# Low halves of the MLP down weights by an accumulating transfer instead of GpSimd subtractions

## The chip, the cores and the metric

The kernel runs on one core of a Trainium2 chip. The metric is the device time of one execution in microseconds; the number for a kernel is the median of its runs.

## The reference, cut to what matters

Two model blocks run in sequence on 512 tokens of width 1024, all in fp32. The first is attention with a gated convolution, a gated feed-forward part and an embedding gate. The second has two layers; each is a mixer (retention in the first, chunked attention in the second) followed by a squared-relu MLP with a hidden width of 4096. The change touches these two MLPs alone:

```
def _sqrelu_mlp(h, w1, w2):
    u = jax.nn.relu(h @ w1)
    return (u * u) @ w2
...
    for i in range(DEPTH_2):
...
        h = h + _sqrelu_mlp(_rmsnorm(h, mlp_norm_g[i]), mlp_w1[i], mlp_w2[i])
```

Every matrix product is made in nearly full fp32 precision out of three products of rounded parts. A number is split into a high part, rounded to fp32r, and a low part, the rest. The kernel adds high times high, high times low and low times high.

## The kernel before, in words

**Chunks and slots.** Weights are streamed in chunks of 1 MB (128 partitions x 2048 columns). Each chunk has a slot, its number modulo 2, in three buffers: `raw` (as loaded), `w_hi` (the high part) and `w_lo` (the low part). Four engines and queues handle a chunk in turn:

- SyncE loads it into `raw` (`load`, L495, issue at L501). It first waits until the low part of the chunk two before, which used the same slot, is made (L498).
- ScalarE copies `raw` to `w_hi`, which rounds it (`split`, L1333, the copy at L1338). It waits for the load and until TensorE has done the group that read the slot before (`two_before`).
- GpSimd subtracts: `w_lo = raw - w_hi`, in four instructions of 512 columns (`lo`, L649, L654). It waits for `w_hi_ready` and counts up `w_lo_ready`.
- TensorE waits for `w_lo_ready` (`chunk_ready`, L715) and makes 48 matmuls of 512 columns: 8 slices of the contraction, 2 output tiles, 3 products (`product`, L738; the matmuls are L729, L730 and L731). With the last of a group it counts up `group_done`.

**The MLP.** A layer's MLP runs over 4 groups (`MLP_GROUPS`), each with 8 chunks. Chunks 0 to 3 are slices of `w1` ("up"): each gives two tiles of the hidden activations, so 8 tiles in all. Chunks 4 to 7 are slices of `w2` ("down"): each contracts all 8 hidden tiles and gives two output tiles, which VectorE adds to `x` (L2039). TensorE's order is `mlp`, L1212. In the first down chunk of a group it waits before each slice k for hidden tile k (`mlp_lo`, L1225).

**ScalarE's order** is written out by hand in `mlp`, L1849. After up group m it splits chunk m + 2, then makes the squares (L1861) and rounds them to the high hidden part (L1864), two tiles each. `down_splits`, L1867, then splits chunks 6 to 9, where 8 and 9 are the up chunks 0 and 1 of the next group. In the last group the splits of chunks 6 and 7 stand between the work for the next norm (L1882 to L1884).

**VectorE** takes relu times the norm factor out of PSUM (L2648) and, after ScalarE, makes the low hidden part by a subtraction (L2652).

**GpSimd's order** is the order of the chunks. From the third chunk of the retention layer on it is one loop over pairs of chunks to the end (L704 to L710):

```
            with pool.Fori(0, after) as i:
                lo(first + 2 * i, first % 2)
                lo(first + 1 + 2 * i, (first + 1) % 2)
```

The waits of one chunk are in the helper `Chunk` (`loads`, `two_before`), those of PSUM in `Group`.

Of the kernel before, what the change touches and what calls it, by code (L numbers as in the profile page):

```python
# [22 lines left out]
F32 = mybir.dt.float32  # L23
F32R = mybir.dt.float32r
I32 = mybir.dt.int32
ALU = mybir.AluOpType
ACT = mybir.ActivationFunctionType
# [33 lines left out]
MLP_GROUPS = 4  # L61
# [80 lines left out]
RET = Phase(GATE, [1, 1, 1, 1, 1, 1, 2, 2], RH)  # L142
MLP_A = Phase(RET, [1] * 8, MLP_GROUPS)

ATT_ORDER = [(kind, g) for kind, g in zip("qkvqkvqkvqkvoooo", (0, 0, 0, 1, 1, 1, 2, 2, 2, 3, 3, 3, 0, 1, 2, 3))]
ATT = Phase(MLP_A, [4 if kind == "o" else 1 for kind, _ in ATT_ORDER])
# [21 lines left out]
class Norm:  # L168
# [39 lines left out]
 ret_v_mean ret_v_lo ret_sq ret_acc ret_var ret_ln ret_rstd ret_ys ret_gate ret_y ret_y_hi ret_y_lo  # L208
 two_s two_mx two_nmx two_exp two_rs two_p two_t two_hi two_lo two_pv two_shift two_o two_ohi two_olo
 gain_pair ffn_old_hi ffn_old_lo apart_done apart_scaled apart_sum gate_old_hi gate_old_lo gate_old_done gate_e_hi gate_e_lo gate_sig gate_read  # L210
 mlp_sq mlp_hi mlp_lo att_in_hi att_in_lo tab_scaled ffn_silu ffn_part fin_tmp fin_t fin_half fin_left fin_right""".split()


def build(nc, T, out):
# [3 lines left out]
    with ExitStack() as ctx:  # L218
# [412 lines left out]
        @block.gpsimd  # L631
        def _(pool):
            pool.memset(ones[:, :], 1.0).then_inc(s["memset_done"], 1)
            pool.memset(eps[:, :], EPS).then_inc(s["memset_done"], 1)

            kr_raw = aux[:, 0, :].rearrange("p (k c) -> p k c", k=KD)
            w_in = T["w_in"][0].rearrange("(k p) c -> p k c", p=P)
            at = Q_RANK + KV_RANK
            pool.wait_ge(s["first_in0"], 32)
            pool.dma_start(tab[:, 0, :].bitcast(I32), bass.AP(T["positions"].tensor, 0, [[0, P], [1, S]]))\  # L640
                .then_inc(s["pos_in"], 16)
            pool.dma_start(freq[:, :], T["c_freq"]).then_inc(s["pos_in"], 16)
            pool.wait_ge(raw_ready[1], MIX.chunk(1).loads)
            for dst, src, n in ((0, 0, 32), (32, 16, 16), (48, 0, 16)):
                pool.dma_start(kr_raw[:, :, dst:dst + n], w_in[:, :, at + src:at + src + n])\
                    .then_inc(s["kr_in"], 16)
            pool.dma_start(ext[:, 255:255 + REL_TABLE], T["att_rel_bias_2"][0]).then_inc(s["ext_in"], 16)

            def lo(number, slot, parts=False, quarters=4):  # L649

                pool.wait_ge(s["w_hi_ready"], number + 1)
                for n in range(quarters):
                    at = slice(n * 512, n * 512 + 512)
                    ins = pool.tensor_tensor(w_lo[:, slot, at], raw[:, slot, at], w_hi[:, slot, at].bitcast(F32),  # L654
                                             ALU.subtract)
                    if parts and n < 3:
                        ins.then_inc(s["w_part"], 1)
                ins.then_inc(s["w_lo_ready"], 1)

            pool.wait_ge(s["w_lo_ready"], 2)  # L660
            lo(MIX.chunk0 + 2, (MIX.chunk0 + 2) % 2)

            pool.wait_ge(s["w_lo_ready"], UQ.chunk0)
            pool.wait_ge(s["w_hi_ready"], UQ.chunk0 + 1)
            for w_lo_part, w_hi_part, raw_part in uq_parts():
                ins = pool.tensor_tensor(w_lo_part, raw_part, w_hi_part.bitcast(F32), ALU.subtract)
            ins.then_inc(s["w_lo_ready"], 1)

            def conv_scaled(half):

                xv = CONV_X[half]
                for m in range(2):
                    pool.wait_ge(pair_free[xv.pair], xv.freed(m))
                    if half == 0 and m == 0:
                        pool.wait_ge(s["r_squared"], 1)
                    u = conv_u[2 * half + m]
                    pool.tensor_tensor(u, u, r_squared, ALU.mult).then_inc(s["conv_ur"], 1)

            for n in range(CONVS.chunks):
                if n == 2:  # L680
                    conv_scaled(0)
                lo(CONVS.chunk0 + n, (CONVS.chunk0 + n) % 2)
                if n == 3:
                    conv_scaled(1)
            lo(WOUT.chunk0, WOUT.chunk0 % 2)
            for m in range(2):
                pool.wait_ge(pair_free[CONV_B[0].pair], CONV_B[0].freed(m))
                pool.tensor_tensor(conv_u[m], conv_u[m], rstd[:, :], ALU.mult).then_inc(s["conv_out0"], 1)
            lo(WOUT.chunk0 + 1, (WOUT.chunk0 + 1) % 2)
            lo(WOUT.chunk0 + 2, WOUT.chunk0 % 2, parts=True)  # L690
            lo(WOUT.chunk0 + 3, (WOUT.chunk0 + 1) % 2)
            lo(PROJ.chunk0, PROJ.chunk0 % 2)
            for n in range(3):
                lo(FFN.chunk0 + n, (FFN.chunk0 + n) % 2, parts=n == 2)
            first = FFN.chunk0 + 3
            before = (FFN_LAST.chunk0 + 6 - first) // 2
            with pool.Fori(0, before) as i:
                lo(first + 2 * i, first % 2)
                lo(first + 1 + 2 * i, (first + 1) % 2)
            for c in range(first + 2 * before, GATE.chunk0 + 4):  # L700
                lo(c, c % 2, parts=c == GATE.chunk0 + 2, quarters=3 if 6 <= c - FFN_LAST.chunk0 < 10 else 4)
            lo(RET.chunk0, RET.chunk0 % 2)
            pool.wait_ge(s["w_lo_ready"], RET.chunk0 + 2)
            first = RET.chunk0 + 2  # L704
            after = (N_CHUNKS - first) // 2
            with pool.Fori(0, after) as i:
                lo(first + 2 * i, first % 2)
                lo(first + 1 + 2 * i, (first + 1) % 2)
            for c in range(first + 2 * after, N_CHUNKS):
                lo(c, c % 2)  # L710


        @block.tensor
# [618 lines left out]
        def _(act):  # L1332
            def split(c, columns=CH):  # L1333

                act.wait_ge(raw_ready[c.slot], c.loads)
                if not c.early:
                    act.wait_ge(s["group_done"], c.two_before)
                act.activation(w_hi[:, c.slot, 0:columns], raw[:, c.slot, 0:columns], ACT.Copy)\  # L1338
                    .then_inc(s["w_hi_ready"], 1)

            def group_ready(g):
                act.wait_ge(s["group_done"], g.done)

# [505 lines left out]
            def mlp(ph, norm, base, next_norm, next_gain):  # L1849
                def up(i, first=False):  # L1850
                    for m in range(4):
                        g = ph.group(m, i)
                        group_ready(g)
                        split(ph.chunk(m + 2, i))
                        if first and m == 0:
                            rsqrt(norm, D)
                        if m:
                            act.wait_ge(s["mlp_lo"], base + i * 8 + 2 * m)
                        for t in range(2):
                            act.wait_ge(pair_free[g.pair], g.freed(t))  # L1860
                            act.activation(tmp[:, t, :], sq[:, t, :], ACT.Square).then_inc(s["mlp_sq"], 1)  # L1861
                        for t in range(2):
                            act.wait_ge(s["mlp_sq"], base + i * 8 + 2 * m + t + 1)
                            act.activation(hid_hi[:, 2 * m + t, :], tmp[:, t, :], ACT.Copy)\  # L1864
                                .then_inc(s["mlp_hi"], 1)

                def down_splits(i):  # L1867
                    for m in range(4):
                        split(ph.chunk(6 + m, i))

                up(0, first=True)
                down_splits(0)
                with act.Fori(1, MLP_GROUPS - 1) as i:
                    up(i)
                    down_splits(i)
                i = MLP_GROUPS - 1
                up(i)
                for m in range(4):
                    g = ph.group(4 + m, i)
                    if next_gain or m < 3:  # L1880
                        group_ready(g)
                    following = ph.chunk(6 + m, i) if m < 2 or next_gain else None  # L1882
                    if following and m < 3:
                        split(following)  # L1884
                    for t in range(2):
                        act.wait_ge(pair_free[g.pair], g.freed(t))
                        if next_gain:
                            gained_hi(next_norm, 2 * m + t, (next_gain[0], next_gain[1] + 2 * m + t))
                        square(next_norm, 2 * m + t, x[:, 2 * m + t, :])
                    if following and m == 3:  # L1890
                        split(following)
# [974 lines left out]
```

## Time and profile before

| | |
|---|---|
| three runs | 1994.1, 1995.39, 1995.42 us |
| median | 1995.39 us |
| profiled execution, span from first to last instruction | 1992.5 us |
| the same with what lies around the span | not recorded apart; the three runs are 1.6 to 2.9 us above the span |
| busy: TensorE, VectorE, ScalarE, GpSimd | 1975.0, 974.1, 782.6, 915.7 us |
| first MLP, about | 1058 to 1400 us of the span |
| second MLP, about | 1643 to 1975 us of the span |

PE is TensorE, PEld its weight loads, DVE VectorE, ACT ScalarE, POOL GpSimd, SP SyncE; a q behind a name is that engine's queue. L12 is line 12 of the kernel. Matmuls are pipelined: a matmul's row lasts 0.39 us while the next one starts 0.22 to 0.23 us after it. Rows of a timeline that stand for several instructions merge them: the duration runs from the first's start to the last's end.

### The profile page before, as it was taken

The numbers are of one execution on the slowest core, as the hardware profiler recorded it, in microseconds if no ns is written. First come the engines' busy times: TensorE is split into PE (matmuls) and PEld (weight loads), VectorE is DVE, ScalarE is ACT, GpSimd is POOL, SyncE is SP. The second block draws the span as 40 slices with busy tenths as digits, with TensorE's granted clock in tenths as the row PEclk, the third lists the DMA queues.
The fourth block names the chain that finished last, engine by engine and source line by source line (L and its number), as shares of the span: only waits on it lengthen the run. The fifth ranks groups of instructions, "written<-read, shape, count | busy, mean of one in ns | idle before, by whom it ended". The sixth has DMA issues, their size and how long they took to land.

```text
span 1992.5 us, 24116 instructions
## 1 busy us (share of the span) xinstructions
PE 1975.0 (99%) x9360; PEld 1640.7 (82%) x9360; DVE 974.1 (49%) x1447; ACT 782.6 (39%) x1137; POOL 915.7 (46%) x662
## 2 busy tenths in 40 slices
PE   8999999999999999999999999999999999999998
PEld 7877878888888888888888888888888888888887
DVE  7667753432358745454555131325466783132234
ACT  7546442321235443434354132233455553223232
POOL 2433555545455344444445454545333345454552
PEclk9999999999999999999999999999999999999999
DMA  5312367375322313232323323233222223323231
GB/s 162 93 49 69 116 94 123 88 101 114 100 90 85 127 64 106 65 104 68 101 66 103 100 90 106 84 105 105 84 84 85 94 74 106 106 85 105 92 98 64
DMA packets 165555, 187.05 MB, mean 94 GB/s; under 512 B 3992, under 2 KB 152224, under 8 KB 165344
## 3 DMA queue, kind: packets, MB, share of 16 engines
q1 hardware_dynamic: 163632, 181.61, 28.6%
q10 hardware_dynamic: 1584, 3.74, 4.2%
q8 instruction: 58, 0.95, 0.2%
q0 software_dynamic: 256, 0.55, 0.1%
q14 instruction: 25, 0.20, 0.0%
HBM read 180.77 MB, written 4.72 MB: 93 GB/s over the span
## 4 chain that ended last, share of the span: by engine, by line
PE 92%; DVE 3%; issue 2%; ACT 1%; POOL 1%; DMA 1%; DVEq 0%; SPq 0%; POOLq 0%; ACTq 0%
PE ps L729 29%; PE ps L730 29%; PE ps L731 29%; PE ps L931 1%; PE ps L901 1%; POOL w_lo L654 1%; PE ps L940 1%; PE ps L941 1%; PE ps L918 1%; ACT w_hi L1338 0%; DMA freq<-in_c_freq 0%; DVE hn_lo L2481 0%; DVE x L2476 0%; DVE scr L1983 0%; ACT scr L1540 0%
## 5 line engine op out<-in xcount | busy, mean ns | idle before, releaser
L654 POOL TENSOR_TENSOR w_lo<-raw,w_hi 128x512 fp32r<-128x512 f32 x636 | 897.1, 1442 | 989.1 <-ACT w_hi L1338 989.1
L729 PE MATMUL ps<-hn_hi,w_hi 128*128 128x512 f32 x1524 | 600.4, 394 | 2.3 <-DVE hn_lo L2328 1.7
L1338 ACT ACTIVATE w_hi<-raw 128x2048 fp32r<-128x2048 f32 (+1 forms) x162 | 308.9, 1907 | 735.5 <-PE ps L731 735.4
L730 PE MATMUL ps<-hn_lo,w_hi 128*128 128x512 f32 x1524 | 593.4, 389 | 0.0
L731 PE MATMUL ps<-hn_hi,w_lo 128*128 128x512 f32 x1524 | 593.4, 389 | 0.0
L730 PE MATMUL ps<-hid_lo,w_hi 128*128 128x512 f32 x904 | 351.7, 389 | 0.0
L729 PE MATMUL ps<-hid_hi,w_hi 128*128 128x512 f32 x888 | 347.0, 391 | 0.1
L731 PE MATMUL ps<-hid_hi,w_lo 128*128 128x512 f32 x888 | 345.6, 389 | 0.0
L729 PEld LDWEIGHTS ps<-hn_hi,w_hi 128*128 128x128 f32 x1524 | 286.2, 188 | 67.4 <-issue 3.5
L731 PEld LDWEIGHTS ps<-hn_hi,w_lo 128*128 128x128 f32 x1524 | 286.1, 188 | 60.4
L730 PEld LDWEIGHTS ps<-hn_lo,w_hi 128*128 128x128 f32 x1524 | 286.3, 188 | 58.9 <-issue 1.4
L2039 DVE TENSOR_TENSOR x<-ps,x 128x512 f32<-128x512 f32 x128 | 82.5, 686 | 278.3 <-PE ps L731 278.2
L730 PEld LDWEIGHTS ps<-hid_lo,w_hi 128*128 128x128 f32 x904 | 169.7, 188 | 35.0 <-issue 0.2
L729 PEld LDWEIGHTS ps<-hid_hi,w_hi 128*128 128x128 f32 x888 | 166.7, 188 | 36.7 <-DVE hid_lo L2428 0.8
L731 PEld LDWEIGHTS ps<-hid_hi,w_lo 128*128 128x128 f32 x888 | 166.7, 188 | 35.0
L2652 DVE TENSOR_TENSOR hid_lo<-scr,hid_hi 128x512 fp32r<-128x512 f32 x64 | 100.9, 1615 | 72.2 <-ACT hid_hi L1864 72.2
L2648 DVE SCALAR_TENSOR_TENSOR scr<-ps,scr 128x512 f32<-128x512 f32 x64 | 41.2, 686 | 154.3 <-PE ps L731 145.4
L2032 DVE TENSOR_TENSOR scr<-ps,scr 128x512 f32<-128x512 f32 x42 | 27.1, 686 | 138.7 <-PE ps L731 135.3
L729 PE MATMUL ps<-w_hi,hn_hi 128*128 128x512 f32 (+1 forms) x256 | 87.0, 340 | 0.2 <-DVE scr L2556 0.2
L730 PE MATMUL ps<-w_lo,hn_hi 128*128 128x512 f32 (+1 forms) x256 | 86.0, 336 | 0.0
L731 PE MATMUL ps<-w_hi,hn_lo 128*128 128x512 f32 (+1 forms) x256 | 86.0, 336 | 0.0
L1983 DVE TENSOR_TENSOR scr<-scr 128x512 f32<-128x512 f32 x65 | 67.3, 1035 | 13.3 <-ACT scr L1358 9.7
(322 smaller groups left out, 1882.9 us busy)
## 6 DMA issues: line engine op xcount, KB each, us to landing
raw<-in_mlp_w SPq DMA_DIRECT2D x64, 1024.0 KB, 5.3
raw<-in_ret_w_in SPq DMA_DIRECT2D x24, 1024.0 KB, 5.1
raw<-in_att_w_in SPq DMA_DIRECT2D x12, 1024.0 KB, 5.2
raw<-in_w_gate SPq DMA_DIRECT2D x11, 1024.0 KB, 5.4
raw<-in_w_up SPq DMA_DIRECT2D x11, 1024.0 KB, 5.3
raw<-in_w_down SPq DMA_DIRECT2D x8, 1024.0 KB, 8.0
raw<-in_ret_w_out SPq DMA_DIRECT2D x8, 1024.0 KB, 5.1
raw<-in_w_in SPq DMA_DIRECT2D x7, 1024.0 KB, 5.7
```

The costliest lines, as they stand in the source:

```text
L654: ins = pool.tensor_tensor(w_lo[:, slot, at], raw[:, slot, at], w_hi[:, slot, at].bitcast(F32), ALU.subtract)
L729: pe.matmul(o, hi, rhs_hi, start=start, stop=False, skip_group_check=True)
L730: pe.matmul(o, hi, rhs_lo, start=False, stop=False, skip_group_check=True)
L731: return pe.matmul(o, lo, rhs_hi, start=False, stop=stop, skip_group_check=True)
L901: ins = pe.matmul(a.score_ps(b, t), q[:, t * P:(t + 1) * P], k[:, 0:(t + 1) * P], start=(n == 0), stop=(n == last), skip_group_check=True)
L918: ins = pe.matmul(a.score_ps(b, t), q[:, t * P:(t + 1) * P], k[:, 0:(t + 1) * P], start=(nth == 0 and n == 0 and t != 0), stop=(nth == 1 a ...
L1338: act.activation(w_hi[:, c.slot, 0:columns], raw[:, c.slot, 0:columns], ACT.Copy)\
L1983: dve.tensor_tensor(ssq, ssq, squares[:, t % 2, :], ALU.add).then_inc(s["norm_acc"], 1)
L2032: dve.tensor_tensor(dst, ps[:, g.bank(m), :], r, ALU.mult).then_inc(pair_free[g.pair], 1)
L2039: dve.tensor_tensor(dst, ps[:, g.bank(m), :], dst, ALU.add).then_inc(pair_free[g.pair], 1)
L2648: dve.scalar_tensor_tensor(sq[:, t, :], ps[:, g.bank(t), :], 0.0, r_bc, ALU.max, ALU.mult).then_inc(pair_free[g.pair], 1)
L2652: dve.tensor_tensor(hid_lo[:, 2 * m + t, :], tmp[:, t, :], hid_hi[:, 2 * m + t, :].bitcast(F32), ALU.subtract)\
```

## The change

For the down chunks (4 to 7 of each MLP group, 32 chunks in all) ScalarE makes two copies: the high part as before, and the high part negated into `w_lo`. GpSimd then issues one transfer that adds `raw` to `w_lo` (1 MB, inside SBUF), waits until it has landed, and counts up `w_lo_ready` itself. Up chunks and all other chunks keep the subtractions. GpSimd's one loop becomes a loop up to the first MLP, the first MLP written out, a loop over the attention layer, and the second MLP written out.

```diff
@@ GpSimd
-            first = RET.chunk0 + 2
-            after = (N_CHUNKS - first) // 2
-            with pool.Fori(0, after) as i:
-                lo(first + 2 * i, first % 2)
-                lo(first + 1 + 2 * i, (first + 1) % 2)
-            for c in range(first + 2 * after, N_CHUNKS):
-                lo(c, c % 2)
+
+            def lo_pairs(first, last):
+
+                with pool.Fori(0, (last - first) // 2) as i:
+                    lo(first + 2 * i, first % 2)
+                    lo(first + 1 + 2 * i, (first + 1) % 2)
+
+            def lo_by_dma(c, nth):
+
+                pool.wait_ge(s["w_hi_ready"], c.number + 1)
+                pool.dma_start(w_lo[:, c.slot, :].bitcast(F32), raw[:, c.slot, :], accum_op=ALU.add)\
+                    .then_inc(s["lo_landed"], 16)
+                pool.wait_ge(s["lo_landed"], 16 * nth)
+                pool.wait_ge(s["w_lo_ready"], c.number)
+                pool.sem_inc(s["w_lo_ready"], 1)
+
+            def mlp_lo(ph, layer):
+
+                for i in range(MLP_GROUPS):
+                    for m in range(4):
+                        lo(ph.chunk0 + m + 8 * i, ph.chunk(m).slot)
+                    for m in range(4):
+                        lo_by_dma(ph.chunk(4 + m, i), 4 * MLP_GROUPS * layer + m + 1 + 4 * i)
+
+            lo_pairs(RET.chunk0 + 2, MLP_A.chunk0)
+            mlp_lo(MLP_A, 0)
+            lo_pairs(ATT.chunk0, MLP_B.chunk0)
+            mlp_lo(MLP_B, 1)
@@ ScalarE
+            def split_negated(c):
+
+                act.wait_ge(raw_ready[c.slot], c.loads)
+                act.wait_ge(s["group_done"], c.two_before)
+                act.activation(w_hi[:, c.slot, :], raw[:, c.slot, :], ACT.Copy)
+                act.activation(w_lo[:, c.slot, :], raw[:, c.slot, :], ACT.Copy, scale=-1.0).then_inc(s["w_hi_ready"], 1)
@@ ScalarE, mlp: after up group m
-                        split(ph.chunk(m + 2, i))
+                        (split if m < 2 else split_negated)(ph.chunk(m + 2, i))
@@ ScalarE, mlp: down_splits
-                        split(ph.chunk(6 + m, i))
+                        (split_negated if m < 2 else split)(ph.chunk(6 + m, i))
@@ ScalarE, mlp: last group
-                        split(following)
+                        (split_negated if m < 2 else split)(following)
```

One semaphore, `lo_landed`, is added to the list.

## Rows read from the trace of the kernel before

**Rows 1.** The page's span, and its busy times of each engine.

```profile
span 1992.5 us, 24116 instructions
...
PE 1975.0 (99%) x9360; PEld 1640.7 (82%) x9360; DVE 974.1 (49%) x1447; ACT 782.6 (39%) x1137; POOL 915.7 (46%) x662
```

**Rows 2.** Busy times by window, the two MLP stages.

```profile
core 0: us, PE busy (x) PEld busy (x) DVE busy (x) ACT busy (x) POOL busy (x), PEclk, DMA share, GB/s
...
1065.00:1410.00 345.00, 345.00 (x1528) 285.77 (x1527) 113.41 (x114) 104.78 (x117) 174.66 (x125) 1.00 0.31 100
...
1650.00:1950.00 300.00, 300.00 (x1325) 248.40 (x1324) 87.82 (x90) 87.39 (x94) 150.34 (x109) 1.00 0.31 98
```

**Rows 3.** Timeline around a chunk border: start us, us, engine, line, what.

```profile
1112.46 0.39 PE L731 MATMUL ps<-hid_hi,w_lo 128*128 128x512 f32 x1
1112.46 0.19 PEld L729 LDWEIGHTS ps<-hid_hi,w_hi 128*128 128x128 f32 x1
1112.68 0.39 PE L729 MATMUL ps<-hid_hi,w_hi 128*128 128x512 f32 x1
...
1112.94 1.92 ACT L1338 ACTIVATE w_hi<-raw 128x2048 fp32r<-128x2048 f32 x1 [8.96 <-PE ps L731]
```

**Rows 4.** Timelines of ScalarE, GpSimd and SyncE's queue, one down chunk; GpSimd beside VectorE.

```profile
1102.07 1.92 ACT L1338 ACTIVATE w_hi<-raw 128x2048 fp32r<-128x2048 f32 x1 [6.86 <-PE ps L731]
...
1104.06 5.02 POOL L654 TENSOR_TENSOR w_lo<-raw,w_hi 128x512 fp32r<-128x512 f32 x4 [4.92 <-ACT w_hi L1338]
...
1109.25 0.37 SPq L501 DMA_DIRECT2D raw<-in_mlp_w  x1
...
1093.20 5.94 POOL L654 TENSOR_TENSOR w_lo<-raw,w_hi 128x512 fp32r<-128x512 f32 x4 [4.94 <-ACT w_hi L1338]
```

**Rows 5.** Timeline of ScalarE, a split and the instruction right behind it.

```profile
1035.90 1.92 ACT L1338 ACTIVATE w_hi<-raw 128x2048 fp32r<-128x2048 f32 x1 [4.36 <-PE ps L731]
1037.72 0.71 ACT L1383 ACTIVATE hn_hi<-x,gains 128x512 fp32r<-128x512 f32 x1
```

**Rows 6.** Timelines of ScalarE and VectorE, chunk 5's split and the last hidden tiles.

```profile
1091.21 1.92 ACT L1338 ACTIVATE w_hi<-raw 128x2048 fp32r<-128x2048 f32 x1 [6.88 <-PE ps L731]
...
1094.72 3.27 DVE L2652 TENSOR_TENSOR hid_lo<-scr,hid_hi 128x512 fp32r<-128x512 f32 x2 [2.30 <-ACT hid_hi L1864]
```

**Rows 7.** Timeline of VectorE, two such subtractions while GpSimd is idle.

```profile
1027.87 1.29 DVE L2606 TENSOR_TENSOR hid_lo<-o_buf,hid_hi 128x512 fp32r<-128x512 f32 x2
```

**Rows 8.** SyncE's loads (L501) in the first MLP: ns min/median/max, and landing.

```profile
L501 SPq DMA_DIRECT2D raw<-in_mlp_w x28: 372/372/373, 1066.0 to 1360.4; - x28
...
DMA to landing us min/median/max: 5.0/5.2/5.8
```

**Rows 9.** DMA queue, 1065 to 1410 us: packets, MB, share of 16 engines.

```profile
q1 hardware_dynamic: 33771, 34.40, 31.4%
```

**Rows 10.** Busy times by short windows after the load issue at 1109.25.

```profile
1109.00:1111.00 2.00, 2.00 (x10) 1.65 (x10) 0.00 (x0) 0.00 (x0) 0.08 (x1) 1.00 0.31 50
1111.00:1113.00 2.00, 2.00 (x11) 1.65 (x10) 0.11 (x1) 0.06 (x1) 0.00 (x0) 1.00 1.01 332
1113.00:1115.00 2.00, 2.00 (x11) 1.65 (x10) 1.18 (x2) 1.86 (x1) 0.06 (x1) 1.00 0.41 143
```

**Rows 11.** DMA issues of the whole run: count, KB each, median us to landing.

```profile
hid_hi<-hid_hi SPq DMA_DIRECT2D x3, 64.0 KB, 2.0
...
aux<-in_w_in POOLq DMA_DIRECT2D x1, 128.0 KB, 3.0
```

**Rows 12.** Timeline of GpSimd, its DMA issues at the start.

```profile
5.92 0.75 POOL L640 DMA_DIRECT2D tab<-in_positions  x1 [4.93 <-DMA raw<-in_w_in]
...
16.47 2.67 POOL L645 DMA_DIRECT2D aux<-in_w_in  x3 [9.26 <-DMA raw<-in_w_in]
```

**Rows 13.** Busy times by window, the first and the last microseconds.

```profile
0.00:6.00 6.00, 0.60 (x3) 0.51 (x4) 0.00 (x0) 1.75 (x3) 0.53 (x7) 1.00 0.66 208
...
1985.00:1992.00 7.00, 0.27 (x3) 0.03 (x1) 2.45 (x4) 1.90 (x4) 0.00 (x0) 0.87 0.75 300
```

More of the change, by code:

```diff
@@ L210 @@
  gain_pair ffn_old_hi ffn_old_lo apart_done apart_scaled apart_sum gate_old_hi gate_old_lo gate_old_done gate_e_hi gate_e_lo gate_sig gate_read
- mlp_sq mlp_hi mlp_lo att_in_hi att_in_lo tab_scaled ffn_silu ffn_part fin_tmp fin_t fin_half fin_left fin_right""".split()
+ mlp_sq mlp_hi mlp_lo lo_landed att_in_hi att_in_lo tab_scaled ffn_silu ffn_part fin_tmp fin_t fin_half fin_left fin_right""".split()
 def build(nc, T, out):
```

## The prediction

> **What bounds the kernel now.** I began with the busy time of each engine [rows 1]: TensorE is busy for 1975.0 us of a span of 1992.5, every other engine for half or less. The table by stage [rows 2] says where the missing 17.5 us lie: not in the two MLP stages. From 1065 to 1410 us TensorE is busy for 345.00 of 345.00 us, from 1650 to 1950 for 300.00 of 300.00, at a granted clock of 1.00 (its 2.4 GHz level). So a faster GpSimd, VectorE or ScalarE can give nothing back inside the MLP stages; the change can only be hidden or cost time, and what decides is how much room each step has before TensorE must wait.
>
> The rhythm is read in the timeline around one chunk border [rows 3, 4]. Matmuls start every 0.2265 us, 48 of them make a chunk, and ScalarE's split starts at 1102.07 and again at 1112.94: one chunk is 10.87 us. With the split's start as zero: the high weights are there at 1.92, GpSimd starts at 1.99 and ends at 7.01, SyncE issues the next load at 7.18. TensorE's first weight load of the next chunk starts at 1112.46, that is at 10.39. GpSimd's four subtractions take 5.02 us there, and 5.94 where VectorE works beside them [rows 4]; the room today is 3.4 us or 2.5 us. Nothing is late now, and the change replaces 5 to 6 us of GpSimd by a second pass of ScalarE and a transfer.
>
> **The change, part by part.** It touches chunks 4 to 7 of each of the 4 groups of each of the 2 MLPs, 32 chunks.
>
> *GpSimd's subtractions go*: 32 times 5.0 to 5.9 us, all of it beside TensorE's work. Worth nothing on the path.
>
> *ScalarE's second pass comes*: another 128x2048 copy of 1.92 us. Two such neighbours on ScalarE overlap a little, the next instruction starts 1.82 us after a split's start [rows 5]. So the negated copy ends at 1.82 + 1.92 = 3.74, and GpSimd, which follows a split's end by 0.07 to 0.08 us [rows 4], issues the transfer at 3.82. What waits behind it on ScalarE: for chunk 5 the squares and high halves of the last up group. They, and VectorE's low halves behind them, move by 1.82 us. Today that chain starts at 1091.21 and ends with VectorE's two subtractions from 1094.72 to 1097.99 [rows 6], 6.8 us after the split's start. TensorE needs the hidden tile 6 after 36 matmuls, and tile 7 after 42, that is 8.15 and 9.5 us into the chunk (times 0.2265), or 7.9 and 9.25 after the split's start, which follows the chunk's first matmul by 0.26 us [rows 3]. With 1.82 us more tile 6 is there at about 7.0 and tile 7 at 8.6. Room of 0.65 us or more is left even at VectorE's present 1.64 us for each, and with GpSimd idle they may fall back to the 0.65 us a piece (1.29 for two) of a stretch where it is idle [rows 7]. Cost nothing. In the down part ScalarE idles 8.96 us before each split [rows 3], which covers the pass.
>
> *The accumulating transfer comes.* It reads 1 MB of raw, reads and writes 1 MB of w_lo. No row shows an adding transfer. The nearest rows are the loads of the same size: in the first MLP 5.2 us from issue to landing, 372 ns of it in SyncE's queue [rows 8]. One load's data pass in 0.62 + 2.02 + 0.82 = 3.5 us of the 16 engines' time (share times 2 us in the three short windows [rows 10]); the queue's 31.4% of 345 us over 34.40 MB gives 3.3 us for 1 MB [rows 9], so some 1.9 us are fixed. The 64 KB copies inside SBUF landed in 2.0 us, so the fixed part is no smaller there [rows 11]. A transfer from GpSimd costs more to issue: 0.75 us and 2.67 us for three, against 0.37; one of 128 KB landed in 3.0 us [rows 11, 12], that is 2.6 fixed after 0.4 of data. I take 2.4. The lower bound has the second read hidden beside the first: 2.4 + 3.3 = 5.7 us. The upper one has three passes in turn, two reads and a write: 2.4 + 9.9 = 12.3 us. I take two passes, since a copy too has one read and one write and shows one pass: 2.4 + 6.6 = 9.0 us.
>
> The Trainium skill (Collectives: The Full Stack, "The bandwidth ceiling") says that a reducing transfer runs at half the rate of a copy, because it needs two source reads on one ring. The load rows bear on it only as the price of a copy. By its own figure for a copy, 31 GB/s per engine, halved and times 16, 1 MB would take an estimated 4.2 us instead of 6.6, and the whole change would come to about 5 us.
>
> *What the room allows.* The transfer must have landed before 10.39, less 0.2 us for two semaphore hops (GpSimd, then TensorE; SyncE takes 0.17 us after GpSimd's end for one [rows 4]): 10.19 − 3.82 = 6.37 us. With 9.0 us the overshoot is 2.63 us.
>
> *How often it is paid.* Not 32 times. There are two slots. If chunk 4 starts 2.63 us late, TensorE is still at it 2.63 us longer, but the split of chunk 5 started when chunk 3 ended, before that wait. GpSimd is free when chunk 4's transfer has landed, 1.9 us into that split (12.82 − 10.87), before the negated copy is done. So chunk 5's transfer starts on time and finds a deadline moved by 2.63 us: no wait. Chunk 6's split starts at the end of chunk 4 and pays again. A pair of chunks costs one overshoot. 16 pairs: 16 × 2.63 = 42 us.
>
> *Loads beside transfers.* SyncE's load for the same slot now waits for the landing. In the second chunk of a pair it is issued 2.1 us after the split's start (12.82 + 0.17 − 10.87) and moves data from 1.15 to 4.6 us later [rows 4, 10], so till 6.7, while the transfer's data start at about 5.3. The overlap is 1.4 us per pair, worth 0 to 22 us in all. I take 0, because two full passes is already the dear side of the two nearest prices. The load itself lands at about 7.3 and is wanted by the next split, at 13.5: hidden. GpSimd's wait has only its own next chunk behind it; after chunk 7 comes an up chunk with 5.0 to 5.9 us of subtraction, started at once or up to the overshoot late, within 10.39.
>
> Sum against the profiled execution: 1992.5 + 42 = 2034.6 us of span. The runs shown are 1994.1 to 1995.42, median 1995.39, 2.9 us over the span, and 1995.39 + 42.1 = 2037.5 us. A measurement of this kernel can tell about 0.2%, 4 us, from no change.
>
> **The rivals.**
>
> *A: the transfer fits.* The second read hides or inner rows of 8 KB move faster than the loads' 1 KB pieces, and landing comes within 6.37 us, or within 0.25 us of it (16 × 0.25 = 4). For it: 5.7 us, the lower bound, is inside. Against it: it asks for almost the time of a plain load with a second megabyte read. Time: 1995.4 us. It ends on the other side: not slower. It decides at 6.37 us of issue to landing. Chance 0.17.
>
> *B: the skill's rate.* 2.4 + 4.2 = 6.6 us (worked from the page named above); by rows alone any price between 6.6 and 7.5 us does the same: 16 × 0.25 to 16 × 1.1, 1999 to 2013 us. Chance 0.16.
>
> *C: dearer than two passes.* With 12.3 us the overshoot is 5.93. Then GpSimd's order bites: chunk 5's transfer can't start before 16.2, lands at 28.5, TensorE ends chunk 4 at 27.2, and the pair costs 7.4 us: 119 us, 2114 us. Still slower adding would make each chunk cost the transfer alone. For it: nothing here shows the adding. Chance 0.14.
>
> *D: the clock falls in the new gaps.* After TensorE stopped at the end, the granted clock of the last 7 us was 0.87, a mix of its two levels, 2.4 and 1.2 GHz; in the first 6 us, with 0.6 us of work, it was 1.00 [rows 13]. Gaps of 2.6 us between 20 us of dense work look like the second. If it fell at each gap for half a chunk, 5.4 us each and 87 us in all would come on top: about 2125 us. Chance 0.03.
>
> *E: faster.* Only stretches with idle TensorE could give, and none of those holds a down chunk. Chance 0.03.
>
> **How the numbers follow.** Two passes, with a landing from 7.5 to 11 us: 0.47, 2013 to about 2080 us. So slower 0.47 + 0.16 + 0.14 + 0.03 = 0.80, same 0.17, faster 0.03. The range goes from A's time with the runs' own spread, 1993, to the three passes, 2115; left out are E's part, half of C and most of D, together under 0.2. The likeliest case alone spans 2013 to 2080.
>
> **What would show it.** In the changed profile: 32 accumulating issues on GpSimd with their time to landing, 9.0 us if right, under 6.4 under A. Splits' starts in the down part 13.5 us apart and 10.9 us apart in turn, not all alike. TensorE's busy time in the first MLP unchanged at 345 us beside about 21 us of idle time, released by GpSimd or its queue. The copies L1338 counted 162 as before plus 32 negated ones of 1.9 us. VectorE's hid_lo subtractions shorter where GpSimd is idle, with no gain from it. The prediction is wrong if the landing is under 6.4 us, if each chunk and not each pair pays, if the loads stretch the transfers by more than 1.4 us, or if the granted clock leaves 1.00.

## The result and the profile after

The changed kernel takes 2009.62 us (median of 4 runs, 2008.16 to 2010.71), the kernel before 1995.41 us beside it: a ratio of 1.007, interval 1.0058 to 1.0082, so 14.2 us slower. Slower was right and 2009.6 lies in the range (a wide one, 1993 to 2115), but the forecast was 2037.5: the loss is a third of the 42 us expected.

The page of the changed kernel: span and busy times (as [rows 1]), the transfers among the costliest groups, and their issues (as [rows 11]).

```profile
span 2007.3 us, 23957 instructions
...
PE 1981.2 (99%) x9360; PEld 1640.3 (82%) x9360; DVE 930.8 (46%) x1447; ACT 839.7 (42%) x1169; POOL 762.4 (38%) x566
...
L714 POOL DMA_DIRECT2D w_lo<-raw x32 | 27.7, 866 | 302.0 <-ACT w_lo L1367 302.0
...
w_lo<-raw POOLq DMA_DIRECT2D x32, 1024.0 KB, 7.0
```

GpSimd lost 153 us of work and VectorE 43; neither shows in the time. TensorE's waits in the changed kernel name the place (who waited for whom: us in total, times, longest):

```profile
PE ps L750 <- POOLq L718: 8.5, 16, 1.7
```

L718 is GpSimd's count-up after the landing. Sixteen waits, not 32: 15 at the first chunk of a pair, and one at a second chunk, whose transfer took 7.6 us. They are 0.5 us each as idle time. The rest of the 14.8 us of span is added busy time, 1981.2 against 1975.0 us: a matmul's row counts 0.39 to 0.50 us on either side of a wait, where a step in the stream is 0.23. The windows of the two MLPs (as [rows 2]) are now short of full by 3.3 and 3.9 us:

```profile
1065.00:1410.00 345.00, 341.74 (x1497) 279.90 (x1496) 90.64 (x113) 131.96 (x129) 95.97 (x76) 1.00 0.54 146
...
1650.00:1950.00 300.00, 296.07 (x1298) 242.79 (x1296) 70.92 (x90) 108.53 (x104) 88.12 (x69) 1.00 0.52 140
```

The timeline of ScalarE shows the rhythm of one group, chunks 4 to 7 and then 8 (only the splits' first copies are copied here):

```profile
1081.25 1.92 ACT L1366 ACTIVATE w_hi<-raw 128x2048 fp32r<-128x2048 f32 x1 [6.88 <-PE ps L752]
...
1092.13 1.92 ACT L1366 ACTIVATE w_hi<-raw 128x2048 fp32r<-128x2048 f32 x1 [5.08 <-PE ps L752]
...
1103.70 1.92 ACT L1366 ACTIVATE w_hi<-raw 128x2048 fp32r<-128x2048 f32 x1 [5.77 <-PE ps L752]
...
1114.58 1.92 ACT L1366 ACTIVATE w_hi<-raw 128x2048 fp32r<-128x2048 f32 x1 [7.16 <-PE ps L752]
...
1126.10 1.92 ACT L1359 ACTIVATE w_hi<-raw 128x2048 fp32r<-128x2048 f32 x1 [7.80 <-PE ps L752]
```

The spacings are 10.88, 11.57, 10.88 and 11.52 us: one late start per pair of chunks, as the prediction's two-slot argument had it. The transfer between them, and where TensorE stands when it lands (timelines of GpSimd and of all engines):

```profile
1107.71 0.86 POOL L714 DMA_DIRECT2D w_lo<-raw  x1 [10.68 <-ACT w_lo L1367]
...
1114.09 0.39 PE L752 MATMUL ps<-hid_hi,w_lo 128*128 128x512 f32 x1
...
1114.78 0.19 PEld L750 LDWEIGHTS ps<-hid_hi,w_hi 128*128 128x128 f32 x1 [0.73 <-POOLq L718]
```

Issue at 4.01 us after the split's start, landing 7.0 later, weight load at 1114.78 − 1103.70 = 11.08 instead of 10.39 [rows 3]: an overshoot of 0.69 us. 16 × 0.69 = 11.0. In the profiled executions the first MLP takes 346.2 us (1059.65 to 1405.84, from the split of chunk 1 to a split behind the last group) against 340.1. The second takes 321.6 us (1650.74 to 1972.33, from the split of chunk 1 to the last split) against 315.3, and what follows the last split takes 1.5 us more: 13.9 us in all. The other 0.9 of the 14.8 us of span lie ahead of the first down chunk; the start varies by such an amount from kernel to kernel (the same split stands between 1058.44 and 1060.61 us in the ten profiles of this study).

What 11.0 leaves of the 13.9 us goes with four late landings of 7.6, 8.3, 7.8 and 7.9 us; the other 28 took 6.9 to 7.0. Beside three of the four the instruction queue moved 16 KB while the transfer was under way, and beside none of the 28; the fourth (7.8 us) follows the one of 8.3, which had moved a load onto it. The DMA queues from 1787.2 to 1795.5 us, the time of the longest one (packets, MB, share of 16 engines):

```profile
q0 software_dynamic: 144, 1.05, 62.5%
q8 instruction: 1, 0.02, 1.1%
```

That the one causes the other is not shown: no run moved the instruction queue's packets, and with the plain copy below one transfer had such company and was on time.

### The profile page after: what moved, and what is told of

Its sections match the earlier page's. It is cut to its first block and busy times, and to the rows that moved or that the text cites. A ratio compares the mean times of both kernels' runs of the same rounds, so it can differ in the third digit from the quotient of the medians.

```text
span 2007.3 us, 23957 instructions
## 1 busy us (share of the span) xinstructions
PE 1981.2 (99%) x9360; PEld 1640.3 (82%) x9360; DVE 930.8 (46%) x1447; ACT 839.7 (42%) x1169; POOL 762.4 (38%) x566
## 5 line engine op out<-in xcount | busy, mean ns | idle before, releaser
L654 POOL TENSOR_TENSOR w_lo<-raw,w_hi 128x512 fp32r<-128x512 f32 x508 | 716.2, 1440 | 849.9 <-ACT w_hi L1359 849.9
L1359 ACT ACTIVATE w_hi<-raw 128x2048 fp32r<-128x2048 f32 (+1 forms) x130 | 247.3, 1902 | 495.8 <-PE ps L752 495.7
L1366 ACT ACTIVATE w_hi<-raw 128x2048 fp32r<-128x2048 f32 x32 | 61.4, 1917 | 196.4 <-PE ps L752 196.4
L714 POOL DMA_DIRECT2D w_lo<-raw x32 | 27.7, 866 | 302.0 <-ACT w_lo L1367 302.0
L2680 DVE TENSOR_TENSOR hid_lo<-scr,hid_hi 128x512 fp32r<-128x512 f32 x64 | 69.1, 1120 | 100.9 <-ACT hid_hi L1892 100.9
```

Of the source, the lines that this page charges most:

```text
L714: pool.dma_start(w_lo[:, c.slot, :].bitcast(F32), raw[:, c.slot, :], accum_op=ALU.add)\
L1366: act.activation(w_hi[:, c.slot, :], raw[:, c.slot, :], ACT.Copy)
L2680: dve.tensor_tensor(hid_lo[:, 2 * m + t, :], tmp[:, t, :], hid_hi[:, 2 * m + t, :].bitcast(F32), ALU.subtract)\
```

## The experiments

Each kernel is compared with the kernel before in the same session. Edits are against the changed kernel.

**Negated copy first.** GpSimd's transfer needs the negated low buffer and raw, not the high buffer. (The semaphore memset_done stands at 2 since the start and is counted on.)

```diff
-act.activation(w_hi[...], raw[...], ACT.Copy)
-act.activation(w_lo[...], raw[...], ACT.Copy, scale=-1.0).then_inc(s["w_hi_ready"], 1)
+act.activation(w_lo[...], raw[...], ACT.Copy, scale=-1.0).then_inc(s["memset_done"], 1)
+act.activation(w_hi[...], raw[...], ACT.Copy).then_inc(s["w_hi_ready"], 1)
...
-pool.wait_ge(s["w_hi_ready"], c.number + 1)
+pool.wait_ge(s["memset_done"], 2 + nth)
 pool.dma_start(w_lo[...], raw[...], accum_op=ALU.add).then_inc(s["lo_landed"], 16)
 pool.wait_ge(s["lo_landed"], 16 * nth)
+pool.wait_ge(s["w_hi_ready"], c.number + 1)
```

> Edit of the changed kernel: ScalarE makes the negated low copy first and the high copy second, and GpSimd issues the transfer after the first of the two; everything else, all 32 transfers included, stays. Theory (the only loss is landing minus room): the issue comes at about 2.0 us after the split's start instead of 4.0, so a landing of 7.0 us ends at about 9.0, inside the 10.2 us of room. No split is spaced 11.5 us any more, TensorE is busy throughout both MLPs, time 1995 to 1997 us. Rival (the transfers disturb TensorE, the loads or the queues by themselves): a part of the 14 us stays, 2002 us or more.

Measured: 1997.46 us, ratio 1.0006 (0.9997 to 1.0015). The changed kernel's 14 us are gone with all 32 transfers in place; only when they start has changed. The windows of the two MLPs (busy times):

```profile
1065.00:1410.00 345.00, 345.00 (x1527) 286.00 (x1526) 90.91 (x114) 133.49 (x133) 98.41 (x77) 1.00 0.55 148
...
1650.00:1950.00 300.00, 299.30 (x1321) 247.68 (x1320) 70.69 (x88) 111.77 (x107) 86.37 (x69) 1.00 0.54 144
```

TensorE is full again, but for two waits behind late landings (median 6.9 us, longest 9.1):

```profile
PE ps L751 <- POOLq L719: 0.9, 2, 0.7
```

The theory holds: the loss was landing minus room.

**Chunks 4 and 6 by transfer, and chunks 4 and 5.** Sixteen transfers each; the other down chunks are subtracted as before the change, and ScalarE negates only where a transfer follows. The second kernel has `m < 2` where the first has `m % 2 == 0`.

```diff
 for m in range(4):
-    lo_by_dma(ph.chunk(4 + m, i), ...)
+    if m % 2 == 0:
+        lo_by_dma(ph.chunk(4 + m, i), ...)
+    else:
+        lo(ph.chunk0 + 4 + m + 8 * i, ph.chunk(4 + m).slot)
```

> Only the first chunk of each pair, 4 and 6, goes by the transfer (16 transfers); 5 and 7 are subtracted by GpSimd as before the change. Theory (a pair of chunks pays one overshoot, the second chunk starts in time): the same loss as with all 32, 16 x 0.69 = 11 us, time 2006 to 2009 us, with splits spaced 11.5 and 10.9 in turn. Rival (each transfer costs its share): half, about 2002 us.

> Only chunks 4 and 5, one pair per group, go by the transfer (16 transfers, as many as with 4 and 6); 6 and 7 are subtracted. Theory (one overshoot per pair): 8 x 0.69 = 5.5 us, 2000 to 2003 us. Rival (each transfer costs the same wherever it stands): the same time as the kernel with chunks 4 and 6.

Measured: with 4 and 6, 2008.33 us, ratio 1.0062 (1.0046 to 1.0077); with 4 and 5, 2002.51 us, ratio 1.0035 (1.0023 to 1.0047). That is 12.4 and 6.5 us over before, for the same number of transfers. TensorE's waits in the two, first 4 and 6, then 4 and 5:

```profile
PE ps L753 <- POOLq L718: 7.6, 16, 1.7
```

```profile
PE ps L753 <- POOLq L718: 3.7, 9, 0.5
```

Half the transfers in the right places cost nearly all of the loss, and half of them packed into pairs cost half. The nine waits are one for each of the eight pairs and one at the second chunk whose transfer again took 7.6 us. The pair pays, not the transfer.

**A plain copy.** The addition is left out, so the low part is not the rest of the weights.

```diff
-pool.dma_start(w_lo[...], raw[...], accum_op=ALU.add)
+pool.dma_start(w_lo[...], raw[...])
```

> The transfer is a plain copy of raw onto the low buffer, of the same size and from the same queue, without the addition (so the low part is wrong and the addition is left out). The term that was mis-sized is the transfer's data part, 5 us instead of 6.6. Theory P (the pass in SBUF is quicker than a load's, and the addition is two such passes): the copy's data take about half of 5 us and it lands in 4.3 to 4.8 us. Rival Q (the pass costs as much as a load's, 3.3 us, and the second read is partly hidden): it lands in 5.2 to 5.5 us. Either way it is inside the room of 6.3 us and the time is that of the kernel before, 1995 to 1997 us.

Measured: 1995.66 us, ratio 0.9999 (0.9989 to 1.0008). Its issues (L714: ns min/median/max) and landings, and its share of the queues from 1065 to 1410 us (16 transfers of 1 MB; packets, MB, share of 16 engines; q1 is SyncE's loads, q0 GpSimd's transfers):

```profile
L714 POOL DMA_DIRECT2D w_lo<-raw x32: 527/528/599, 1084.2 to 1964.4; - x32
...
DMA to landing us min/median/max: 4.4/4.5/6.4
...
q1 hardware_dynamic: 33817, 34.45, 31.5%
q0 software_dynamic: 2304, 16.78, 12.6%
```

The same three views of the changed kernel:

```profile
L714 POOL DMA_DIRECT2D w_lo<-raw x32: 859/859/929, 1085.3 to 1976.3; - x32
...
DMA to landing us min/median/max: 6.9/7.0/8.3
...
q1 hardware_dynamic: 32880, 33.49, 29.8%
q0 software_dynamic: 2304, 16.78, 24.1%
```

12.6% of 345 us in 16 parts is 2.7 us of data for a copy, 24.1% is 5.2 us for an addition: 1.9 times the copy. Taken from the landings of 4.5 and 7.0 us, both leave 1.8 us, called the fixed part here. So theory P was right: doubling was the right rule, the price of a pass and the fixed part were not. The Trainium skill's half rate (Collectives: The Full Stack, "The bandwidth ceiling") is what the trace shows, 24.1 against 12.6; its 31 GB/s per engine, given there for a collective's ring, is not: 1 MB in 2.7 us on 16 engines is 24 GB/s.

**Half the columns added.** The low part of the other half is left out.

```diff
-pool.dma_start(w_lo[:, c.slot, :]..., raw[:, c.slot, :], accum_op=ALU.add)
+pool.dma_start(w_lo[:, c.slot, 0:1024]..., raw[:, c.slot, 0:1024], accum_op=ALU.add)
```

> Only the first 1024 of the 2048 columns are added; the low part of the other half is left out. Landing time at half the size. If the fixed part is 1.8 us and the data part 5.2 us for 1 MB: 4.4 us. If the fixed part is the predicted 2.4 us with 4.6 us of data: 4.7 us. Inside the room either way: 1995 to 1997 us.

Measured: 1996.2 us (one run). Landings, and the queue's share from 1065 to 1410 us:

```profile
DMA to landing us min/median/max: 4.5/4.5/5.8
...
q0 software_dynamic: 2304, 8.39, 12.8%
```

12.8% for 16 half transfers is 2.8 us each: 1.7 us fixed, against 1.8 for the whole transfer. The two expectations, 4.4 and 4.7, are too near each other for the landing alone to decide; the share does.

**Two halves, pipelined.** ScalarE makes high and negated parts of one half, then of the other; GpSimd issues a transfer behind each and waits for both at the end.

```diff
+for h in range(2):
+    at = slice(h * 1024, h * 1024 + 1024)
+    act.activation(w_hi[:, c.slot, at], raw[:, c.slot, at], ACT.Copy)
+    act.activation(w_lo[:, c.slot, at], raw[:, c.slot, at], ACT.Copy, scale=-1.0)\
+        .then_inc(s["w_hi_ready" if h else "memset_done"], 1)
```

> ScalarE works by halves of 1024 columns (high, negated, high, negated) and GpSimd issues a transfer behind each half, without waiting between them. Theory: the first half is issued at about 2.1 us and its data are done by 6 us, the second is issued at about 4.1 and lands 4.4 us later, or at most 1 us more behind the first: 8.5 to 9.5 us, inside the room of 10.2. No loss, 1995 to 1998 us, the same as with the negated copy first. Rival (each transfer has a cost of its own, 64 issues of 0.9 us and 64 landings): a part of the 14 us stays or it gets more, 2003 us or over.

Measured: 1996.26 us, ratio 1.0003 (0.9994 to 1.0012). A second way to start earlier removes the loss as well, with 64 issues instead of 32; no price of the transfers themselves shows as long as they land in time. Neither repair beats the kernel before.

**Two halves in turn.** This gives the forecast its own conditions: a landing of about 9 us.

```diff
+for h in range(2):
+    at = slice(h * 1024, h * 1024 + 1024)
+    pool.dma_start(w_lo[:, c.slot, at]..., raw[:, c.slot, at], accum_op=ALU.add).then_inc(s["lo_landed"], 16)
+    pool.wait_ge(s["lo_landed"], 32 * nth - 16 + 16 * h)
```

> The transfer is made in two halves of 1024 columns, the second issued only when the first has landed. This puts a landing of about the predicted 9.0 us in place of 7.0: two times 1.8 us fixed and 2.6 us of data, 8.9 us with the wake-up between. Theory (a pair pays one overshoot, loads beside transfers cost little): overshoot 2.6 us, splits spaced 13.5 and 10.9 us in turn, 16 x 2.6 = 42 us, time 2036 to 2040 us. Rival (at this size each chunk pays, or the loads stretch the second transfer of each pair by the overlap of 1.4 us): 2060 us or more for all 32, or 2050 to 2060 us with spacings of 13.5 and 12. Rival (the clock falls in gaps of 2.6 us): a granted clock under 1.00 in the MLPs and over 2060 us.

Measured: 2074.68 us, ratio 1.0384 (1.0368 to 1.04): 79 us, not 42. The theory fails here, and both rivals have their part. Timeline of GpSimd, issues of chunk 4's two halves, chunk 5's two halves:

```profile
1084.24 0.93 POOL L716 DMA_DIRECT2D w_lo<-raw  x1 [6.97 <-ACT w_lo L1369]
1089.15 0.88 POOL L716 DMA_DIRECT2D w_lo<-raw  x1 [3.98 <-DMA w_lo<-raw]
1095.10 0.86 POOL L716 DMA_DIRECT2D w_lo<-raw  x1 [5.07 <-ACT w_lo L1369]
1101.79 0.86 POOL L716 DMA_DIRECT2D w_lo<-raw  x1 [5.83 <-DMA w_lo<-raw]
```

Chunk 4's first half takes 4.9 us to the next issue, chunk 5's takes 6.7: its landing is 6.4 us instead of 4.5, beside a load that SyncE issued at 1093.93, when chunk 4 had landed. Timeline of TensorE at that landing, and windows from there on (the granted clock is the third figure from the end):

```profile
1090.59 0.39 PE L754 MATMUL ps<-hn_hi,w_lo 128*128 128x512 f32 x1
1093.82 0.50 PE L752 MATMUL ps<-hid_hi,w_hi 128*128 128x512 f32 x1 [2.85 <-POOLq L720]
```

```profile
1094.00:1096.00 2.00, 2.00 (x7) 1.64 (x8) 0.00 (x0) 2.00 (x4) 0.86 (x1) 0.72 0.45 114
1096.00:1098.00 2.00, 2.00 (x6) 1.54 (x6) 1.29 (x2) 0.89 (x2) 0.00 (x0) 0.50 1.03 350
1098.00:1100.00 2.00, 2.00 (x10) 1.60 (x9) 0.00 (x0) 0.00 (x0) 0.00 (x0) 0.93 1.10 245
```

After a gap of 2.85 us the granted clock is 0.72, 0.50 and 0.93 in the next three windows: 1.2 GHz for part of the chunk, and 6 matmuls in 2 us instead of 10 or 11. The page's span and busy times, and TensorE's waits:

```profile
span 2074.8 us, 23989 instructions
...
PE 2000.9 (96%) x9360; PEld 1651.9 (80%) x9360; DVE 930.7 (45%) x1447; ACT 839.4 (40%) x1169; POOL 790.3 (38%) x598
...
PE ps L752 <- POOLq L720: 56.0, 24, 4.3
```

The span is 82.3 us longer than before: 56.0 us are these waits, and 25.9 us are added busy time. Most of the latter is the clock: its mean over the run is 0.988 instead of 0.999, and 0.011 × 2075 = 23 us. The four runs bear this out: with a mean clock of 0.988 they take 2076.6 and 2075.6 us, with 0.991 2073.8, with 0.993 2068.1.

Of the 24 waits, 16 are at the first chunk of a pair, 44.2 us in all, and 8 at the second, 11.8 us. The clock fell at nine of the 16 first waits. The seven pairs without a fall all had a second wait, and of the nine with a fall only one had. That fits slow matmuls giving a late second transfer its time: the stretched transfer and the slow clock hide each other in part, and a price worked out for each alone can't be added.

The fall does not follow every gap: after the next long one no window is under 1.00 (timeline, then windows).

```profile
1120.18 0.50 PE L752 MATMUL ps<-hid_hi,w_hi 128*128 128x512 f32 x1 [2.55 <-POOLq L720]
```

```profile
1120.00:1122.00 2.00, 1.82 (x8) 1.51 (x9) 0.00 (x0) 1.45 (x1) 0.26 (x1) 1.00 0.31 50
1122.00:1124.00 2.00, 2.00 (x11) 1.65 (x10) 0.00 (x0) 0.00 (x0) 0.60 (x1) 1.00 0.97 306
```

The length of the gap alone does not decide it: of the gaps in this run one of 2.70 us was followed by a fall and one of 2.91 us was not.

**Negated first, and halves in turn.** Both edits, for an overshoot between the changed kernel's 0.7 us and the 2.9 us of the halves in turn.

> Both edits at once: the negated copy first (issue at 2.0 us) and the transfer in two halves in turn (landing 9.0 us after the issue, 4.5 measured for each half). The last landing is at 11.1 us against the room of 10.2: an overshoot of 0.9 us, between the 0.7 of the changed kernel and the 2.9 of the halves in turn. Theory (one overshoot per pair, nothing else at this size): 16 x 0.9 = 14 us, 2009 to 2012 us, granted clock 1.00, splits' spacing 11.8 and 10.9 in turn. Rival (the second transfer of each pair now starts 1.8 us earlier than in the changed kernel, on top of the load issued at the first one's landing, as where a first half landed in 6.4 us instead of 4.5): 1.9 us more per pair, 30 us more, about 2040 us, with landings of over 6 us among the first halves.

Measured: 2057.25 us, ratio 1.0303 (1.0286 to 1.032), 61 us over before. Theory wrong by 47 us, the rival right in kind and 17 us short. GpSimd's timeline, first and second halves of chunks 5, 6 and 7:

```profile
1093.52 0.86 POOL L716 DMA_DIRECT2D w_lo<-raw  x1 [5.11 <-ACT w_lo L1369]
1100.14 0.86 POOL L716 DMA_DIRECT2D w_lo<-raw  x1 [5.75 <-DMA w_lo<-raw]
1105.69 0.86 POOL L716 DMA_DIRECT2D w_lo<-raw  x1 [4.70 <-ACT w_lo L1369]
1113.64 0.86 POOL L716 DMA_DIRECT2D w_lo<-raw  x1 [7.09 <-DMA w_lo<-raw]
1118.71 0.86 POOL L716 DMA_DIRECT2D w_lo<-raw  x1 [4.21 <-DMA w_lo<-raw]
1126.87 0.86 POOL L716 DMA_DIRECT2D w_lo<-raw  x1 [7.30 <-DMA w_lo<-raw]
```

A first half that meets the load takes 6.6, 8.0 and 8.2 us to the next issue instead of 4.9. Once chunk 5 is late through this, chunk 6's transfer meets a load too, so it spreads from one chunk in two to three in four, and TensorE now waits 31 times:

```profile
PE ps L753 <- POOLq L721: 47.3, 31, 2.6
```

It is a loop: a late landing makes the load late, the late load lies on the next transfer and makes that one late. The DMA queues show in what way. From the issue at 1118.71 to 1123.3 us only the load moves data, and the half transfer's data all pass from there to 1126.6 (packets, MB, share of 16 engines; first the one window, then the other):

```profile
q1 hardware_dynamic: 924, 0.95, 78.0%
```

```profile
q0 software_dynamic: 144, 0.52, 80.2%
q1 hardware_dynamic: 116, 0.10, 9.5%
```

So the transfer starts late more than it runs slowly: its data begin at least 4.6 us after the issue, where they begin about 1.5 us after it when no load is under way (the issue at 1082.66). Why the load goes first was not tried.

The clock fell here too, in four places (mean 0.996), and behind shorter waits than in the kernel with the halves in turn alone. Timeline and window:

```profile
1738.51 0.67 PE L753 MATMUL ps<-hid_hi,w_hi 128*128 128x512 f32 x1 [1.88 <-POOLq L721]
```

```profile
1738.50:1742.50 4.00, 3.99 (x11) 3.15 (x12) 0.00 (x0) 1.93 (x2) 0.86 (x1) 0.57 0.63 152
```

## Why the prediction was wrong

- **No gain in the MLPs; GpSimd's and VectorE's relief worth nothing.** Right: GpSimd 153 us less, VectorE's hid_lo subtractions 1120 ns on average where they were 1615 by the two pages, no time from either.
- **ScalarE's second pass costs nothing by itself.** Right: with it in place and the transfer in time, 1.0006 and 0.9999.
- **Room of 6.37 us for the landing.** Right: the issue was put at 3.82 us and came at 4.01, the hops at 0.2 and came at about 0.1, so 10.39 − 4.01 − 0.1 = 6.3.
- **"I take two passes ... 2.4 + 6.6 = 9.0 us."** This is the term that failed. The landing takes 7.0 us, 1.8 fixed and 5.2 data. Two passes was right (1.9 times a copy). A pass was priced by the loads, 3.3 us, and costs 2.6 to 2.7 inside SBUF; the fixed part was raised from 1.9 to 2.4 for GpSimd's longer issue and stayed at 1.8. 2.0 us too much, on a landing of which only the excess over 6.3 us counts, turned 0.69 into 2.63, and 11.0 us of loss into 42. The direction was no luck, for the wait stands where it was said to; the size was wrong.
- **"A pair of chunks costs one overshoot."** Right, shown by the spacings, by 16 waits, and by the kernels with 4 and 6 (12.4 us) and with 4 and 5 (6.5 us). 16 × 0.69 = 11.0 of the 14.2 us; what is left goes with four late landings (8.3 us the longest, a wait of 1.7 us) and the start's own scatter.
- **"Loads beside transfers ... I take 0."** Right only because the overshoot is small: with landings of 7.0 us one transfer of 32 met most of a load, the one of 7.8 us. With a landing of 9.0 us the load adds 1.9 us to the second landing of a pair, more than the bound of 1.4, and TensorE waits for it in eight pairs of 16.
- **The clock, chance 0.03.** It stays at 1.00 in both MLPs of the changed kernel, but with gaps of about the forecast's size it falls at nine of 16. With 9.0 us of landing the kernel takes 2075 us, not 2037.5: the forecast's size was wrong a second time, by two terms put at nothing, whose cost the true landing hid.
- **Rival B** (landing of 6.6 to 7.5 us, 1999 to 2013 us) is what happened, and had 0.16. A row was there for the fixed part: the 64 KB copies inside SBUF landed in 2.0 us [rows 11], about 1.8 without their 0.2 us of data. The prediction read it as a floor and took the dearer GpSimd row.
- **Two slips in its sums**, which do not move the forecast: a landing of 11 us gives 16 × 4.63 = 74 us, so about 2070 us where it says 2080, and a landing of 6.6 us gives 16 × 0.23 = 4 us where it says 5.

## What to carry to other kernels

When a wait is taken against a deadline, only the excess counts: work out the deadline to 0.1 us first, then ask what the uncertainty of the priced step does to the excess, and spread the forecast over it. Check the order of the instructions ahead of a slow step: here its input was made last for no reason, and making it first gave the loss back, to within what the runs can tell. With two buffers a late item is forgiven every second time, but beyond a point lateness feeds itself, through loads that start on its landing and through the clock.

## What the runs showed of the hardware

- An accumulating transfer of 1 MB inside SBUF lands in 7.0 us, a plain one in 4.5, an accumulating one of half the size in 4.5: 1.7 to 1.8 us fixed, 2.7 us per MB copied, 5.2 per MB added. The issue on GpSimd takes 859 ns with the addition and 527 ns without.
- A load of 1 MB from HBM beside an accumulating half transfer stretched it from 4.5 to 6.4 us, and in the last experiment up to 8.4 (the longest landing), more than the load's own 3.3 us of data. Where it was looked at, the transfer's data began at least 4.6 us after the issue instead of about 1.5.
- TensorE's granted clock fell to 0.50 at nine of the 16 gaps ahead of a pair's first chunk (1.4 to 4.3 us) with the halves in turn, and at four of 31 gaps of at most 2.6 us in the last experiment, one of them 1.88 us long; the 16 gaps of at most 1.7 us in the changed kernel brought no fall. Gaps have to be priced with a chance for each.
